# ScalarE rounds two weight units between the two norm roots of the mixers instead of behind both

## What is computed

```python
for l in range(DEPTH_2):
    p = jnp.einsum('bsd,dc->bsc', x, w_in[l])
    ...
    y_a = _mla(c_q, c_kv, k_r, cos, sin, mla_q_norm[l], mla_kv_norm[l], mla_w_uq[l], mla_w_ukv[l])
    y_b = _mlstm(m_q, m_k, m_v, m_o, m_g, mlstm_gate_bias[l], mlstm_norm[l])
    y_c = _ssd(s_z, s_xbc, s_dt, ssd_conv_w[l], ssd_conv_b[l], ssd_dt_bias[l],
               ssd_a_log[l], ssd_d[l], ssd_norm[l])
    heads = jnp.concatenate([y_a.astype(dtype), y_b.astype(dtype), y_c.astype(dtype)], -1)
    mix = jnp.einsum('bsc,cd->bsd', heads, w_out[l])
    x = _layernorm(DEEPNORM_ALPHA * x + mix, ln1_g[l], ln1_b[l]).astype(dtype)
```

## Time and profile before

| what | value |
|---|---|
| median of 3 runs | 1423.39 us (1422.11 to 1429.92) |
| the profiled execution: its own time | 1421.55 us |
| the profiled execution: span from first to last instruction | 1419.1 us |
| TensorE matmuls busy | 1314.1 us (93% of the span) |
| VectorE busy | 849.3 us (60%) |
| ScalarE busy | 734.1 us (52%) |
| GpSimd busy | 635.2 us (45%) |
| mean granted TensorE clock | 0.96 of full speed |

### The profile page before, as it was taken

How to read it: one execution, slowest core, us unless ns; L and a number is a source line. 1 busy time by engine, 2 the same in 40 slices (tenths; PEclk the granted TensorE clock), 3 DMA queues, 4 the chain that set the end, 5 groups by cost and what they waited for, 6 DMA issues and landing times.

```text
span 1419.1 us, 17480 instructions
## 1 busy us (share of the span) xinstructions
PE 1314.1 (93%) x6096; PEld 1069.0 (75%) x6096; DVE 849.3 (60%) x1345; ACT 734.1 (52%) x1090; POOL 635.2 (45%) x522
## 2 busy tenths in 40 slices
PE   6899988999999899999998869999989897899996
PEld 3687767888886688887787758888768775778884
DVE  7574763354244544114676667777777946777777
ACT  4343444454564444445566416666645652466664
POOL 2899899987667689997301310000060023000000
PEclk9999999999999899999999979999989989799998
DMA  9966468655443555554531007878844300577772
GB/s 380 364 228 237 148 227 286 255 218 208 151 152 132 187 178 177 177 202 153 208 119 61 0 20 297 314 286 318 307 162 151 117 1 0 216 287 285 286 305 89
DMA packets 44476, 279.86 MB, mean 197 GB/s; under 512 B 5453, under 2 KB 8781, under 8 KB 12014
## 3 DMA queue, kind: packets, MB, share of 16 engines
q1 hardware_dynamic: 37426, 263.82, 50.5%
q10 hardware_dynamic: 6974, 15.05, 2.9%
HBM read 274.66 MB, written 4.19 MB: 197 GB/s over the span
## 4 chain that ended last, share of the span: by engine, by line
PE 72%; DVE 13%; POOL 6%; DMA 3%; DVEq 3%; ACT 2%; issue 2%; SPq 0%; ACTq 0%; POOLq 0%
PE G L1135 11%; PE G L1137 11%; PE G L1136 11%; PE AC L1135 8%; PE AC L1137 8%; PE AC L1136 8%; POOL w_lo L604 6%; DVE mod L1957 2%; DMA rel_scratch<-arena 1%; DMA w_raw<-w_stream 1%; DVE w_lo L1870 1%; PE T L1233 1%; DVE arena L2457 1%; PE G L1676 1%; DVE sm L1906 1%
## 5 line engine op out<-in xcount | busy, mean ns | idle before, releaser
L604 POOL TENSOR_TENSOR w_lo<-w_raw,w_hi 128x512 fp32r<-128x512 f32 (+1 forms) x480 | 608.0, 1300 | 374.9 <-ACT w_hi L660 367.1
L660 ACT ACTIVATE w_hi<-w_raw 128x1024 fp32r<-128x1024 f32 x448 | 470.1, 1055 | 388.7 <-PE G L1137 193.3
L1870 DVE TENSOR_TENSOR w_lo<-w_raw,w_hi 128x1024 fp32r<-128x1024 f32 x230 | 278.3, 1223 | 65.0 <-ACT w_hi L660 57.0
L1135 PE MATMUL AC<-w_hi,yT_hi 128*128 128x512 f32 x464 | 183.7, 396 | 8.6 <-POOL w_lo L604 6.7
L1135 PE MATMUL G<-w_hi,xT_hi 128*128 128x512 f32 x432 | 179.5, 416 | 1.7 <-DVE xT_lo L1876 1.7
L1136 PE MATMUL AC<-w_lo,yT_hi 128*128 128x512 f32 x464 | 180.8, 390 | 0.0
L1137 PE MATMUL AC<-w_hi,yT_lo 128*128 128x512 f32 x464 | 180.8, 390 | 0.0
L1136 PE MATMUL G<-w_lo,xT_hi 128*128 128x512 f32 x432 | 172.9, 400 | 0.0
L1137 PE MATMUL G<-w_hi,xT_lo 128*128 128x512 f32 x432 | 172.8, 400 | 0.0
L1135 PE MATMUL G<-w_hi,arena_r 128*128 128x512 f32 x320 | 128.0, 400 | 3.9 <-DVE arena L2707 3.4
L1137 PE MATMUL G<-w_hi,arena_r 128*128 128x512 f32 x320 | 125.1, 391 | 0.0
(11 more groups left out here) (446 smaller groups left out, 1778.6 us busy)
## 6 DMA issues: line engine op xcount, KB each, us to landing
w_raw<-w_stream SPq DMA_DIRECT2D x152, 1024.0 KB, 4.9
w_raw<-w_expert SPq DMA_DIRECT2D x96, 1024.0 KB, 4.9
mod<-rows ACTq DMA_DIRECT2D x2, 2048.0 KB, 8.8
rel_scratch<-arena ACTq DMA_DIRECT2D x1, 3072.0 KB, 20.7
mod<-rows ACTq DMA_DIRECT2D x3, 476.0 KB, 5.6
x_sb<-x SPq DMA_DIRECT2D x1, 1024.0 KB, 9.5
arena<-const SPq DMA_DIRECT2D x1, 1024.0 KB, 8.2
mod<-gn_g ACTq DMA_DIRECT2D x1, 1024.0 KB, 12.7
```

What stands on the lines that cost most here:

```text
L604: i = pool.tensor_tensor(w_lo[:, k % SLOTS, cols], w_raw[:, raw, cols], w_hi[:, k % SLOTS, cols].bitcast(F32), ALU.subtract)
L660: act.activation(w_hi[:, k % SLOTS, cols], w_raw[:, raw, cols], ACT.Copy).then_inc(hi_ready, 1)
L1135: pe.matmul(out, xh, wh, start=start, stop=False)
L1870: dve.tensor_tensor(w_lo[:, k % SLOTS, :], w_raw[:, k % RAW, :], w_hi[:, k % SLOTS, :].bitcast(F32), ALU.subtract).then_inc(lo_ready, 1)
```

## The change

In the step q = 1 of `down_his` ScalarE first does the first root, then the second, then rounds units 4 and 5. After the change it rounds them between the two roots. The call in `down_his` is skipped for that step through a new argument, `done_at`. Nothing is added or taken away: in both layers the same instructions stand in another order, on ScalarE alone.

```diff
-            def down_his(n, k, t, pairs, after=None, end=None):
+            def down_his(n, k, t, pairs, after=None, end=None, done_at=None):
...
-                    if q >= 1:
+                    if q >= 1 and q != done_at:
                         his(k + 2 * (q - 1) + SLOTS, min(k + 2 * q + SLOTS, end or k + 2 * q + SLOTS), n)
...
                     if q == 1:
                         root(r + 2, sm[:, 64:72])
+                        his(L_OUT + SLOTS, L_OUT + SLOTS + 2, n)
                         root(r + 3, sm[:, 72:76])
...
-                down_his(n, L_OUT, t + LT_OUT, 4, gate_and_roots, L_MOE)
+                down_his(n, L_OUT, t + LT_OUT, 4, gate_and_roots, L_MOE, 1)
```

## The result

The changed kernel took 1415.28 us as the median of 4 runs (1414.41 to 1418.73), the kernel before 1423.56 beside it (4 runs, 1422.11 to 1429.92). The ratio is 0.9947, with a 95% interval of 0.9928 to 0.9965: faster, by just over the 0.5% that I had called the edge of what can be told. The profiled execution has a span of 1416.8 us, with TensorE busy for 1312.1.

The account below looks back on a forecast made before the run. The prediction took the output projection to hang on GpSimd's late start on remainders. A gain of 1.8 us in each of two layers, 3.6 in all, took 1423.39 to 1419.8 us, in a range of 1415.5 to 1424.

Parts of the forecast that it names:

- the norm chain: VectorE, output projection: taking turns at the ports with GpSimd makes it end at 812.30 instead of 810.37, 1.93 us lost.
- the variance with one operand: VectorE, line 1892 before: taken to wait nothing for GpSimd; at the full price of 0.69 us, 1.1 per layer would remain.
- Rival 1: VectorE's 512-column instructions are not blocked by GpSimd: 3.3 us gained per layer, time 1416.8; chance 0.12.
- Rival 2: GpSimd keeps the ports while it has work, VectorE's 2575 ends 5.2 us late: 2.3 lost per layer, 1428.0; chance 0.04.
- Rival 3: Gain lost downstream, by a longer low clock or unit 5 holding up the second root: 1422 to 1424; chance 0.11.
- the wait before pair 3's turn: TensorE, output projection: a new wait of about 1 us, put down to VectorE's later norm chain.
- The wait for unit 7: TensorE, output projection: the 1.72 us wait for GpSimd's remainder goes, and unit 7 starts at 819.6 instead of 821.38.
- the term of the sum: Output projection: unit 7 and the residual sum behind it come 1.8 us earlier per layer, 3.6 in all.
- the 0.5% that I gave 0.86: Whole time: a chance of 0.86 that the change stays within about 0.5%, 7.1 us, of the kernel before.
- the clock's part: TensorE's clock gate: 1.3 us a layer can come or go; its mean was put at nothing, 1.3 in the range.
- The tie that I had forecast: VectorE's 2572 at 803.79 against GpSimd's first at 803.80; if GpSimd goes first, 1.6 us per layer remain.

Follow-up runs that it names:

- e3: Changed kernel, but GpSimd makes only one column of the remainders of units 4 and 5, others left stale; stages 16.28 and 16.26 us, ratio to before 0.9950.
- e4: Changed kernel, but only unit 4 is rounded between the two roots, unit 5 right behind the second; stages 18.24 and 18.26 us, ratio to before 0.9969.
- e5: Changed kernel with each remainder of units 4 and 5 as one GpSimd instruction of 128 x 1024; stages 19.76 us in both layers, ratio to before 0.9979.
- e8: A follow-up run which the text does not tie to one version; its variance instruction took 0.17 us.
- e1: The changed kernel again with no edit, beside the kernel before; stages 17.81 and 17.82 us, median 1416.94 us over 10 runs, ratio 0.9968.
- e10: The changed kernel once more with no edit, beside the kernel before; stages 17.82 and 17.80 us, ratio 0.9943 over 6 runs.

## Why the prediction was right, and where its sizes were off

**ScalarE.** This was right. Unit 4 starts 0.11 us behind the first root. Unit 5 starts 2.05 behind it in the first layer and 2.69 in the second, since it follows the end of pair 0; 2.45 was forecast, from where pair 0 ended in the trace of before. The second root was never held up by it.

**The lock between GpSimd and VectorE.** Right in kind and nearly in size. Counted from the first root's start, the norm chain ends at 9.77 us; 9.80 was forecast, and it was 7.87 before. But two terms inside this sum were wrong and cancelled, so that its closeness is partly luck. I put the variance with one operand (now 1893) at no cost, because 1864 had waited for none; but 1864 has one operand in PSUM, and the variance has it in SBUF. It took 0.48 instead of 0.17, so 0.31 of a price that I had bounded at 0.69. It is 0.47 to 0.48 in all three profiles of the changed kernel, 0.34 beside eighths, and 0.17 wherever GpSimd is idle at that moment (`e3`, `e4`, `e5`, `e8`). Against it, 2589 was to wait 0.3 for the ports and found them free (0.70). The Trainium skill, "SBUF — State Buffer", section "Who interferes with whom", spoke against this change by a lock for VectorE instructions with two SBUF inputs: the trace agrees, with 1.06 to 1.17 against 0.69, and `e3` shows the lock's cost as 1.5 us a layer. That they take turns by instruction was read from the earlier trace rows; the three grains show it.

**Rivals.** Rival 1 (no blocking; 3.3 a layer) is out as a forecast for this kernel, but `e3` shows its stage when the lock is removed: 3.6. Rival 2 (GpSimd keeps the ports) is out: VectorE's 2576 lost 0.37, not 5. Its fear comes true when one instruction is a whole unit, with 1.99 lost at once. Rival 3 (the gain is lost downstream) did not occur.

**TensorE.** Unit 4 was to start 0.09 later against the root and started 0.01 later; the wait before pair 3's turn was forecast near 1 and is 0.96. The wait for unit 7 is gone. Unit 7 starts 1.96 earlier (forecast 1.8) and the residual sum 2.08 and 2.02 earlier. So the term of the sum was mis-sized by 0.25 us a layer, 4.1 in place of 3.6: unit 4 gave 0.08 of it, unit 7 0.08 more, and the residual sum another 0.1 behind it. That last 0.1 is a cost of waiting that the sum left out: behind the wait of before, the first matmul of unit 7 took 0.50 us and the next started 0.34 later; now it takes 0.39 and the next starts 0.23 later.

**The total.** This is where the forecast missed, and the reason is known in part only. Three comparisons of the changed kernel, weighted by their intervals, give 0.9957 ± 0.0010, or 6.2 us (4.7 to 7.6). That is 0.43%, inside the 0.5% that I gave 0.86, while the first comparison alone, at 0.53%, was just outside it; it was the middle one of the three. The stages account for 4.1.

I fitted the 196 executions of all kernels that are compared here with one offset for each kernel and one common slope on the time at the low granted clock (2 x (1 - mean clock) x span). The slope is 0.45 us per us and the residual 1.9 us. At equal clock the changed kernel is 4.25 ± 0.95 us faster, which is what its stages show, and the other versions agree with their stages within their intervals too, but for whole units and for the old order with VectorE (7.0 ± 1.6 against 4.8). The remaining 2 us or so goes with a mean granted clock of 0.9617 (20 runs) against 0.9601 (89 runs) before. The step that failed is the one that put the mean of the clock's part at nothing. The range had the same fault: I allowed 1.3 us a layer for the clock, but took 1.3 once from its lower end; with both layers it would have started at 1414.2. Most other versions also came out 1 to 4.5 us better than their stages; before against itself and the one without the remainders did not.

The profiles show where the rest lies. The table has the time up to the first layer's first root, the time between the two stages (from the first layer's residual sum to the second layer's first root) with its granted clock, and the time behind the second layer's residual sum:

| profile | up to the stages | between | clock there | behind |
|---|---|---|---|---|
| before | 802.50 | 352.79 | 0.93 | 224.05 |
| before, again | 801.92 | 352.86 | 0.93 | 224.05 |
| changed | 807.66 | 349.46 | 0.95 | 224.02 |
| changed, `e1` | 802.29 | 350.26 | 0.94 | 224.02 |
| changed, `e10` | 804.38 | 351.51 | 0.94 | 223.89 |
| second layer only | 802.66 | 352.91 | 0.93 | 224.01 |
| remainders 4, 5 left out | 804.40 | 352.79 | 0.93 | 223.97 |
| unit 4 only | 803.81 | 349.46 | 0.95 | 224.03 |

Behind the second stage all agree, as I had assumed. Between the stages I was wrong: the changed kernel takes 2.4 us less on the mean of its three profiles, with the same work at a higher clock, and 4.1 + 2.4 is about the 6.2 of the whole. What decides the clock there stays open. A shorter first stage alone does not bring the gain, for the version without the remainders has the shortest stage in the table and takes as long there as before. The time up to the stages, in which nothing was changed, moves by more than this from one execution to the next: the one late start in the table, 807.66, goes with a granted clock of 0.97 up to there, all others with 0.98. Whole executions of the kernel before took 1417.1 to 1429.9. The twelve small matmuls of the earlier trace rows show only this scatter. In both profiles of before they took 1.55 us in the first layer and 2.83 (2.82) in the second, in the first profile of the changed kernel it is the other way round, in `e1` they took 1.55 in both layers and in `e10` 2.83 in both. TensorE's timeline of the first:

```profile
795.42 2.82 PE L1685 MATMUL G<-arena 128*128 128x64 f32 x12 [1.52 <-POOL arena L639]
...
1164.61 1.55 PE L1685 MATMUL G<-arena 128*128 128x64 f32 x12 [1.52 <-POOL arena L639]
```

Whole units, with 0.2 us in their stages and 3.5 ± 1.1 at equal clock, can be explained by the low clock inside their stages. It is on there for about 3.5 us in each layer (from the 0.91), for which the fit allows 3.2 us in all, while it cost some 0.5 in each stage. With this put right both come to about 1.2 or 1.3, by an estimate from one profile.

The Trainium skill, "TensorE: Matmul & The Clock Gate", section "What's actually happening", says that the window by which the clock gate is set runs free and does not start anew with the kernel. The scatter between executions agrees with that, but a shift of the mean would not follow from it.

## What to carry to other kernels

When a queue is reordered so that GpSimd starts earlier, ask what VectorE does in that time. In a stretch of two-operand SBUF instructions on the path, each one can pay up to about one GpSimd instruction (here 0.37 to 0.48 us each, beside instructions of 0.7), so the grain decides, and moving the work to VectorE behind its critical chain can be worth more than the reordering. Read a gain of a few microseconds from the stage in the trace, between two events that the change does not touch, since whole executions scatter by more than ten. A removed wait is worth only the distance to what is late next: here 1.11 us before unit 4 turned into a wait for the norm, and only the 1.72 before unit 7 came off.

## What the runs showed of the hardware

- A VectorE instruction of 128 x 512 with two SBUF operands that had to wait took 0.79 to 0.84 us beside GpSimd instructions of 128 columns, 1.06 to 1.26 beside 256, and 2.10 or 2.68 beside 1024; alone it took 0.69.
- A VectorE `tensor_scalar` of only 128 x 4 waited too (0.48 instead of 0.17), while a reciprocal of the same size (0.18) and a reduction of 128 x 512 (0.69) did not.
- When both came up almost at once, the first had the ports: 2573 at 808.94 kept its 0.69 and GpSimd's at 808.96 took 1.26; in `e4` GpSimd's at 812.16 was first (0.74) and the norm instruction at 812.19 took 1.26. The tie that I had forecast with 0.01 us between the two came out that way round with 0.02.
- The start of this stage moved by more than 5 us between executions of the same kernel (802.29 and 807.66).
- The first matmul behind a wait of TensorE took longer: 0.50 us behind 1.72 us of waiting, 0.39 where there was none, at the same granted clock of 1.00.
- After a wait of 2.58 us for VectorE, TensorE's granted clock fell to 0.68 over the next 4 us (812 to 816 in `e5`), and matmuls of 128 x 512 took 0.63 us instead of 0.39.
